# Stick-breaking attention: the sums over later keys as one-pass matmuls of two parts of softplus instead of fp32 matmuls

## The reference

```
log_beta = log_sigmoid(z)
log_fail = where(strict, log_sigmoid(-z), 0)          # = -softplus(z)
between  = cumsum over later keys of log_fail, without the key itself
w        = where(strict, exp(log_beta + between), 0)
out      = w @ v
```

## Time and profile before

| | before |
|---|---|
| time, median of 3 runs (lowest to highest) | 2039.21 us (2038.03 to 2041.23) |
| span of the profiled execution (its own time outside the span is not recorded) | 2036.8 us |
| PE busy | 1991.7 us, 98% |
| DVE busy | 1166.4 us, 57% |
| ACT busy | 1049.5 us, 52% |
| PE's share of the chain that ended last | 93% |
| first stick-breaking mixer, PE work from about 210 to 343 us | |
| second stick-breaking mixer, the same about 1499 us later | |

### The profile page before, as it was taken

How to read it: one execution, slowest core, us unless ns; L and a number is a source line. 1 busy time by engine, 2 the same in 40 slices (tenths; PEclk the granted TensorE clock), 3 DMA queues, 4 the chain that set the end, 5 groups by cost and what they waited for, 6 DMA issues and landing times.

```text
span 2036.8 us, 26261 instructions
## 1 busy us (share of the span) xinstructions
PE 1991.7 (98%) x9408; PEld 1648.0 (81%) x9408; DVE 1166.4 (57%) x1636; ACT 1049.5 (52%) x1601; POOL 50.6 (2%) x106
## 2 busy tenths in 40 slices
PE   7999999999999999999999998999999999999998
PEld 5888778888888878788888887888888888778887
DVE  4555655555655585555565557565556556546554
ACT  5444545544544465644454446554455445535443
POOL 2000000000100000000000000000000000000000
PEclk9999999999999999999999999999999999999999
DMA  6555432655555553455555544255556555425553
GB/s 211 190 187 181 162 124 83 206 185 186 186 186 185 166 179 121 155 186 185 185 186 186 185 148 137 85 166 185 187 171 199 186 188 183 144 84 165 185 185 114
DMA packets 242712, 342.21 MB, mean 168 GB/s; under 512 B 11981, under 2 KB 194906, under 8 KB 242650
## 3 DMA queue, kind: packets, MB, share of 16 engines
q1 hardware_dynamic: 242272, 341.34, 51.8%
q10 hardware_dynamic: 378, 0.02, 0.0%
HBM read 340.27 MB, written 1.05 MB: 168 GB/s over the span
## 4 chain that ended last, share of the span: by engine, by line
PE 93%; DVE 3%; ACT 3%; DMA 1%; issue 0%; SPq 0%; POOLq 0%; POOL 0%; ACTq 0%; DVEq 0%
PE psum L424 83%; PE psum L572 2%; DVE wlo L411 2%; ACT whi L397 1%; PE psum L806 1%; PE psum L455 1%; PE psum L757 1%; PE psum L824 1%; PE psum L1413 1%; PE psum L707 0%; PE psum L761 0%; PE psum L768 0%; DMA raw<-in_ffn_wi 0%; PE psum L827 0%; PE psum L1387 0%
## 5 line engine op out<-in xcount | busy, mean ns | idle before, releaser
L411 DVE SCALAR_TENSOR_TENSOR wlo<-raw,gains,whi 128x512 fp32r<-128x512 f32 (+2 forms) x900 | 611.8, 743 | 357.5 <-ACT whi L397 357.4
L424 PE MATMUL psum<-whi,xT_hi 128*128 128x512 f32 (+1 forms) x1960 | 778.1, 397 | 20.7 <-DVE wlo L411 7.1
L424 PE MATMUL psum<-whi,xT_lo 128*128 128x512 f32 (+1 forms) x1960 | 763.9, 390 | 0.0
L424 PE MATMUL psum<-wlo,xT_hi 128*128 128x512 f32 (+1 forms) x1960 | 761.7, 389 | 0.0
L397 ACT ACTIVATE whi<-raw,gains 128x512 fp32r<-128x512 f32 (+2 forms) x900 | 570.1, 708 | 70.2 <-PE psum L424 64.5
L424 PEld LDWEIGHTS psum<-whi,xT_hi 128*128 128x128 f32 x1960 | 369.3, 188 | 95.2 <-DVE wlo L411 19.2
L424 PEld LDWEIGHTS psum<-whi,xT_lo 128*128 128x128 f32 x1960 | 368.8, 188 | 77.6
L424 PEld LDWEIGHTS psum<-wlo,xT_hi 128*128 128x128 f32 x1960 | 369.7, 189 | 70.8
L407 DVE TENSOR_TENSOR wlo<-raw,whi 128x2048 fp32r<-128x2048 f32 x100 | 229.2, 2292 | 139.2 <-ACT whi L393 139.2
L393 ACT ACTIVATE whi<-raw 128x2048 fp32r<-128x2048 f32 x100 | 191.5, 1915 | 185.8 <-PE psum L424 185.8
L424 PE MATMUL psum<-whi,hidT_hi 128*128 128x512 f32 x640 | 249.7, 390 | 0.0
(11 more groups left out here) (176 smaller groups left out, 861.4 us busy)
## 6 DMA issues: line engine op xcount, KB each, us to landing
raw<-in_ffn_wi SPq DMA_DIRECT2D x352, 512.0 KB, 4.6
raw<-in_ffn_wo SPq DMA_DIRECT2D x176, 512.0 KB, 4.2
raw<-in_sb_w_in SPq DMA_DIRECT2D x48, 512.0 KB, 4.6
raw<-in_ml_w_in SPq DMA_DIRECT2D x24, 512.0 KB, 4.5
raw<-in_sb_w_out SPq DMA_DIRECT2D x16, 512.0 KB, 4.1
raw<-in_ml_w_out SPq DMA_DIRECT2D x8, 512.0 KB, 4.4
raw<-in_mla_w_out SPq DMA_DIRECT2D x8, 512.0 KB, 4.0
raw<-in_mla_w_in SPq DMA_DIRECT2D x4, 512.0 KB, 4.4
```

Of the source, the lines that this page charges most:

```text
L411: last = dve.scalar_tensor_tensor(wlo[:, slot, r], raw[:, slot, r], gain_col(p.gain + k), hi[:, r], op0=ALU.mult, op1=ALU.subtract)
L424: m = pe.matmul(dst, a, b[:, slot, cols], start=first and n == 0, stop=last and n == 2)
```

## The change

The fp32 matmuls with the triangle and the square become fp32r matmuls, one pass each, and softplus is given to them in two parts, as the weights are. ACT copies softplus, rounded, to `sp_hi` (`softplus_high`), DVE subtracts that from softplus into `sp_lo` (`softplus_rest`), and PE multiplies the constants with `sp_hi` and with `sp_lo`. `softplus` itself now overwrites `sb_e`, and `sb_sp` is gone. `sp_hi` and `sp_lo` are single buffers: `softplus_high(g)` waits until remainder(g-1) has read them. The constants are made in fp32 on POOL and copied to fp32r.

```diff
-        neg_tri = sb("neg_tri", [P, P])
-        neg_ones = sb("neg_ones", [P, P])
+        tri_work = sb("tri_work", [P, 2, P])
+        neg_tri = sb("neg_tri", [P, P], F32R)
+        neg_ones = sb("neg_ones", [P, P], F32R)
+        sp_hi = sb("sp_hi", [P, 3 * NCOL], F32R)
+        sp_lo = sb("sp_lo", [P, 3 * NCOL], F32R)
...
             def remainder(g):
-                bank, sp3 = SB_Z[g], sb_sp[:, g % 2, :]
-                pe.wait_ge(sp_done, 4 * s.inst + g + 1)
-                for b in range(3):
-                    pe.matmul(psum[:, bank + b, :], neg_tri[:, :], sp3[:, b * NCOL:(b + 1) * NCOL], start=False,
-                              stop=b == 2, skip_group_check=True)
...
+                bank = SB_Z[g]
+                pe.wait_ge(sp_lo_done, 4 * s.inst + g + 1)
+                for sp3 in (sp_hi, sp_lo):
+                    for b in range(3):
+                        pe.matmul(psum[:, bank + b, :], neg_tri[:, :], sp3[:, b * NCOL:(b + 1) * NCOL], start=False,
+                                  stop=b == 2, skip_group_check=True)
+                    for b in range(2):
+                        i = pe.matmul(psum[:, bank + b, :].rearrange("p (a n) -> p a n", a=2)[:, :, P:SEQ], neg_ones[:, :],
+                                      sp3[:, 2 * NCOL + b * SEQ:2 * NCOL + (b + 1) * SEQ].rearrange("p (a n) -> p a n", a=2),
+                                      start=False, stop=True, skip_group_check=True)
                 i.then_inc(r_done, 1)
...
+            def softplus_high(g):
+                act.wait_ge(sp_done, 4 * s.inst + g + 1)
+                if g:
+                    act.wait_ge(r_done, 4 * s.inst + g)
+                act.activation(sp_hi[:, :], sb_e[:, g % 2, :], ACT.Copy).then_inc(sp_hi_done, 1)
+
...
             copies(2)
+            softplus_high(0)
             conv(9)
             weights(0)
...
             conv(12)
+            softplus_high(1)
             weights(1)
             conv(13)
             log1p(2)
+            softplus_high(2)
             y_split(act, s, 0, 3)
             y_split(act, s, 1, 7)
             conv(14)
             weights(2)
             log1p(3)
+            softplus_high(3)
             conv(15)
             weights(3)
...
-                dve.scalar_tensor_tensor(sb_sp[:, g % 2, :], banks3(SB_Z[g]), 0.0, sb_e[:, g % 2, :],
-                                         op0=ALU.max, op1=ALU.add).then_inc(sp_done, 1)
+                e = sb_e[:, g % 2, :]
+                dve.scalar_tensor_tensor(e, banks3(SB_Z[g]), 0.0, e, op0=ALU.max, op1=ALU.add).then_inc(sp_done, 1)
+
+            def softplus_rest(g):
+                dve.wait_ge(sp_hi_done, 4 * s.inst + g + 1)
+                dve.tensor_tensor(sp_lo[:, :], sb_e[:, g % 2, :], sp_hi[:, :].bitcast(F32), ALU.subtract).then_inc(sp_lo_done, 1)
...
             softplus(0)
             conv(9)
+            softplus_rest(0)
             evac(3)
...
             softplus(1)
+            softplus_rest(1)
             conv(12)
...
             softplus(2)
             evac(5)
+            softplus_rest(2)
             y_split(dve, s, 0, 3)
             y_split(dve, s, 1, 7)
             conv(14)
             absolute(3)
             softplus(3)
+            softplus_rest(3)
             conv(15)
             heads(2)
...
-            pool.memset(neg_ones[:, :], -1.0)
-            link(pool.memset(neg_tri[:, :], -1.0))
+            link(pool.memset(tri_work[:, :, :], -1.0))
...
+            pool.tensor_copy(neg_tri[:, :], tri_work[:, 0, :])
+            pool.tensor_copy(neg_ones[:, :], tri_work[:, 1, :])
```

More of the change, by code:

```diff
@@ L175, in trunk @@
         sb_e, at = carve(at, 2, 3 * NCOL)
-        sb_sp, at = carve(at, 2, 3 * NCOL)
         mqT, at = carve(at0, 4, SEQ)
@@ L256, in trunk @@
         sp_done = sem("sp_done")
+        sp_hi_done = sem("sp_hi_done")
+        sp_lo_done = sem("sp_lo_done")
         r_done = sem("r_done")
@@ L1747, in _ @@
             pool.memset(ones[:, :], 1.0)
-            pool.memset(neg_ones[:, :], -1.0)
-            link(pool.memset(neg_tri[:, :], -1.0))
-            link(pool.affine_select(out=neg_tri[:, :], in_=neg_tri[:, :], compare_op=ALU.is_ge, fill=0.0, base=0,
+            link(pool.memset(tri_work[:, :, :], -1.0))
+            link(pool.affine_select(out=tri_work[:, 0, :], in_=tri_work[:, 0, :], compare_op=ALU.is_ge, fill=0.0, base=0,
                                     pattern=[[-1, P]], channel_multiplier=1))
+            pool.tensor_copy(neg_tri[:, :], tri_work[:, 0, :])
+            pool.tensor_copy(neg_ones[:, :], tri_work[:, 1, :])
             link(pool.tensor_copy(ident_b[:, :], ident[:, :]))
```

## The result

The changed kernel takes 2058.65 us (median of 4 runs, 2057.05 to 2060.31) against 2039.1 us before; the ratio is 1.0095, with a 95% interval of 1.0082 to 1.0108. It is slower by 19.5 us, where 13 were forecast, and 1.1 us above the upper end of the range. Direction and mechanism are as forecast; one term, the clock's, is not. One execution of the kernel before, among those that stood beside later kernels, took 3392.8 us at a mean clock of 0.557; it is left out of the comparisons.

A forecast was written before the change was run, and what follows sets the result against it. PE was taken to bound the kernel. Span 2036.8 + 7.5 (waits less saving) + 5.6 (clock falls) = 2049.9, plus 2.4 from span to median, gave 2052.3 us, 0.6% slower; range 2045.0 to 2057.5.

The forecast's parts named there:

- What bounds the kernel, and what is late next: Whole kernel: PE bounds it, busy 98% of the span; in the mixers it would newly wait for softplus's second part.
- five waits: PE's waits per mixer: remainder(0) 5.1 us, remainder(1) 0.4, y_fill(1) 2.8 (1.3 of it new), remainder(3) 1.95, y_fill(2) 1.1.
- The price of waits less saving: Per mixer, groups 0 to 3: +3.6 - 1.1 - 0.2 + 1.45 = +3.75 us, +7.5 for both.
- What PE saves: At each remainder: 1.93 us instead of 3.44, so 1.5 us shorter, 12 us for all eight.
- TensorE's clock: Behind PE's new or longer mixer waits: the clock falls to half, costing 1.87 us each time, 5.6 us in all.
- 3 x 1.87 = 5.6 us: Three clock falls: one behind each remainder(0) wait, one for the pair of waits at y_fill(1).
- its upper bound: The clock term's highest case: six falls, also counting both y_fill(1) waits and group 3 in both mixers, 11.2 us.
- fewer falls: Rival: the mixers' waits come as worked out but the clock stays up, 2046.7 us; chance 25%.
- faster: Rival: all eight remainders find their operand ready and the 12 us are kept, 2027 us; chance 5%.
- no change: Rival: waits sum to about 6 us per mixer and no clock falls, 2035 to 2043 us; chance 5%.
- four-pass matmuls: Rival: remainder's 256-column matmuls are not one pass, 1.2 us more per remainder, 9.3 in all, 2061.6 us; chance 4%.
- below 6.0 us of new waits per mixer it gains: Break-even for the mixers: the change gains below 6.0 us of new waits per mixer; 9.8 were worked out.

The follow-up runs named there:

- fill_all: Changed kernel with matmuls of zeros laid under PE's waits ahead of remainder(0), y_fill(1) and remainder(3), 39 per mixer: 2046.4 us, ratio 1.0039.
- save_only: Kernel before, with one-pass remainder matmuls using softplus's high part twice; no ACT copy, no DVE subtraction: 2034.0 us, ratio 0.9969.
- last_waits: Changed kernel with mended orders at groups 0 and 2, remainder(3) and y_fill(2) inside output piece 13, evac(4) split around softplus(1): 2027.4 us, ratio 0.994.
- shift: Kernel before, with 8 matmuls of zeros (1.83 us) at the start of the SwiGLU two sublayers ahead of the latent mixer: 2044.4 us, ratio 1.002.
- before_again: Kernel before, unchanged, profiled once more: that execution took 2041.8 us.
- all_orders_fill: Changed kernel with mended orders at groups 0 and 2, remainder(3) inside piece 13, and 11 matmuls of zeros under the evac(1) wait: 2034.4 us, ratio 0.9972.

## Why the prediction was right and where it failed

- *What bounds the kernel, and what is late next*: right for four of the five waits, which came at the place and, within 0.1 us, in the length worked out: 5.02, 0.31, 2.77, 1.87. The fifth, 1.1 us at y_fill(2), came only in fill_all (0.82); in the changed kernel the half clock kept PE at remainder(3) until its operand was there. The price of waits less saving was +3.75 per mixer; fill_all, with the clock up, shows +3.96 and +3.98.
- *What PE saves*: right within 0.2 us. A remainder at full clock is 0.98 + 0.23 + 0.69 + 0.23 = 2.1 us with its start behind a wait; without, fill_all's remainder(2) takes 0.69 + 0.23 + 0.69 + 0.23 = 1.84. 1.93 was forecast. (Its own bounds, 0.11 and 0.19 us for a 256-column matmul, give a saving of 1.3 to 1.6, not 1.4 to 1.6.) The copy took 1.49 and the subtraction 1.75 us.
- *TensorE's clock*: the step that failed is the term "3 x 1.87 = 5.6 us". The clock accounts for 4.1 us in the first mixer (146.55 against fill_all's 142.46), 7.4 in the second (148.30 against 140.86) and 1.65 in the latent mixer, 13.2 in all. What was wrong is the number of half-clock stretches, not the price of one.
  - At the new or longer waits six were there and three were counted: one behind each long wait, as forecast, but one behind both waits at y_fill(1), where one of the two was counted, and one at each remainder(3), which the sum left out and only its upper bound held. Priced in the first mixer, from the end of the wait on and against fill_all: remainder(0) and piece 8 take 9.55 us against 7.59, 1.96 more; y_fill(1), remainder(2) and scores(3) 7.36 against 5.78, 1.58 more; remainder(3) to the end of piece 13 9.63 against 9.08, only 0.55 more, since the slow remainder(3) covers the wait at y_fill(2). None of the three costs much more than the 1.87 that was taken; in the second mixer the long one costs 2.4. (The stretch at a long wait lasts 6.8 us, but begins in the wait.) Together that is 4.1 and 4.4 us per mixer, 8.5 in place of 5.6, and by that alone the working gives 2055.2, inside the range.
  - What took it out of the range: the sum held the falls at waits that the change doesn't touch to be fixed. They are not. The second mixer's evac(1) wait and the latent mixer added 3.1 + 1.65 us, which no bound of mine took in. With 5.6 replaced by 13.2 the working gives 2059.9; 2058.65 was measured.
- *Rivals*: fewer falls, faster, no change and four-pass matmuls are all refuted, the last by save_only. The point "below 6.0 us of new waits per mixer it gains" was not tested as a number. last_waits, with one new wait of 1 us, does gain.
- Not settled: which execution gets which falls. The time of the kernel before goes by its mean clock: of the executions that stood beside the second set of kernels sixteen took 2037.1 to 2039.2 us at 0.998, three 2040.8 to 2042.0 at 0.996 or 0.997 and five 2043.2 to 2043.7 at 0.995. All falls in the profiles stand in or behind waits of PE, but an equal wait has one or has none. shift makes it likely that the moment at which the code comes shares in deciding it; why these moments and not others, no run tells.

## What to carry to other kernels

Cheaper matmuls on the bounding engine were worth 1.6 us per group, and two operand-preparing steps, put in the queues where the code reads well, took back more. Before adding a producer step to an in-order engine, look up what stands ahead of it there, and what waits behind it: one conversion ahead of the subtraction was worth 15.7 us, 10 of them the wait itself. And when TensorE is the bound, price a new wait at its length plus the half-clock stretch behind it (here up to 2.4 us), and keep a few us of the range for falls that move into unchanged code.

## What the runs showed of the hardware

- Between the first mixer and the end of PE's work the twelve profiles of this study (before, before_again, the changed kernel and the nine others) have 41 stretches of half clock. Each begins in a wait of PE or behind one; the shortest of these waits is 1.46 us. By the length of the wait: both of 5.02 us had one, all six of 1.87 to 1.92, 22 of 30 of 2.76 or 2.77, two of 12 of 2.26 to 2.31, and nine of 62 of 1.46 to 1.66. So the length alone doesn't decide. A stretch lasted 3.4 or 6.8 us. The Trainium skill (TensorE: Matmul & The Clock Gate, section "Why this matters for your kernels") warns of idle gaps between bursts of matmuls. The two waits of 5.02 us agree with it; many of the shorter ones had a fall as well.
- TensorE can be kept at full clock through a wait by multiplying zeros: 39 such matmuls per mixer made the program 12 us shorter (fill_all). A like filling elsewhere (all_orders_fill) gained nothing; its median was 5 us longer.
- Work of 1.83 us added to one place cost 5.5 us in the median (shift), and the latent mixer's unchanged code took 302.5 to 307.5 us in different kernels: of a change in the time of this program some 0.2% can come from such falls alone.
